# Low parts of weights on GpSimd, and gates, scan and query rows moved ahead, in the first block's input runs

## The reference, cut to what matters

```python
hn = rms_norm(h, norm_mix_g[l])
q, k, v, xr, gate = jnp.split(hn @ w_in[l], splits, axis=-1)      # five parts of 512 columns
q = apply_partial_rope(rms_norm(q, q_norm_g[l]), cos, sin)        # per head of 64; k alike
o_attn = diff_attention(q, k, v, lam)
xc = conv(xr)                                                     # width 4, causal
r = sigmoid(xb @ w_rg + b_rg); i = sigmoid(xb @ w_ig + b_ig)      # the two gates, in blocks of 64
a = exp(8 * r * log_sigmoid(lru_L))
u = sqrt(max(-expm1(2 log a), 0)) * i * xc
y = scan(a, u)                                                    # y[t] = a[t] * y[t-1] + u[t]
o_rec = rms_norm(y * gelu(gate), rec_norm_g[l])
h = h + concat(o_attn, o_rec) @ w_out[l]
```

## Time and profile before

| | us |
|---|---|
| median of 3 runs | 1753.96 (1753.67 to 1758.41) |
| the profiled execution | 1755.41 |
| its span | 1752.6 |
| TensorE busy, matmuls | 1629.3 (93%) |
| VectorE busy | 1014.0 (58%) |
| ScalarE busy | 843.1 (48%) |
| GpSimd busy | 21.0 (1%) |
| mean granted TensorE clock | 0.961 |

### The profile page before, as it was taken

One profiled execution on the slowest core, in us unless ns is written; L12 is line 12 of the kernel. 1 busy time (PEld: TensorE's weight loads), 2 busy tenths in 40 slices (PEclk: granted clock), 3 DMA queues, 4 the chain that ended last, 5 costly groups with the idle time before them and its releaser, 6 DMA issues.

```text
span 1752.6 us, 27456 instructions
## 1 busy us (share of the span) xinstructions
PE 1629.3 (93%) x11494; PEld 1421.4 (81%) x11494; DVE 1014.0 (58%) x1621; ACT 843.1 (48%) x1410; POOL 21.0 (1%) x38
## 2 busy tenths in 40 slices
PE   6978999989898999999989899999999798989997
PEld 6947999989578999887657778888887674779997
DVE  7675645465856555724453665325554666577575
ACT  6744434448445444534563454224432446556563
POOL 0000000000000000310000000000000000000000
PEclk9989999999898999999999899999999898989998
DMA  7445545353455463771102451232223520244632
GB/s 286 145 182 191 197 147 210 131 196 144 169 205 205 142 219 146 214 228 73 72 1 73 169 198 68 92 135 96 74 83 121 216 97 1 72 181 153 228 144 91
DMA packets 60522, 253.84 MB, mean 145 GB/s; under 512 B 4976, under 2 KB 8304, under 8 KB 42480
## 3 DMA queue, kind: packets, MB, share of 16 engines
q1 hardware_dynamic: 59088, 248.95, 38.6%
q0 software_dynamic: 1312, 3.15, 0.9%
HBM read 251.03 MB, written 1.05 MB: 144 GB/s over the span
## 4 chain that ended last, share of the span: by engine, by line
PE 63%; DVE 3%; ACT 2%; issue 1%; DVEq 0%; ACTq 0%
PE PA L849 49%; PE PA L910 2%; PE PA L911 2%; PE PB L1206 2%; PE PA L920 1%; PE PB L1193 1%; PE PB L790 1%; DVE small L1913 1%; PE PA L1379 1%; PE PA L1278 1%; PE PA L883 1%; PE PA L884 1%; PE PA L889 1%; DVE tmp L1613 1%; PE PB L979 1%
## 5 line engine op out<-in xcount | busy, mean ns | idle before, releaser
L1423 DVE TENSOR_TENSOR WL_t<-raw,WH_t 128x1024 fp32r<-128x1024 f32 (+1 forms) x344 | 444.5, 1297 | 370.1 <-ACT WH_t L2044 369.8
L849 PE MATMUL PA<-XH_t,WH_t 128*128 128x256 f32 (+2 forms) x1984 | 632.6, 319 | 8.4 <-issue 4.4
L849 PE MATMUL PA<-XL_t,WH_t 128*128 128x256 f32 (+2 forms) x1984 | 626.5, 316 | 0.0
L849 PE MATMUL PA<-XH_t,WL_t 128*128 128x256 f32 (+2 forms) x1984 | 626.3, 316 | 0.0
L2044 ACT ACTIVATE WH_t<-raw 128x1024 fp32r<-128x1024 f32 (+1 forms) x344 | 381.3, 1113 | 206.9 <-PE PA L849 171.2
L849 PEld LDWEIGHTS PA<-XH_t,WH_t 128*128 128x128 f32 x1984 | 379.3, 191 | 40.5 <-issue 14.6
L849 PEld LDWEIGHTS PA<-XL_t,WH_t 128*128 128x128 f32 x1984 | 379.5, 191 | 21.5 <-issue 0.5
L849 PEld LDWEIGHTS PA<-XH_t,WL_t 128*128 128x128 f32 x1984 | 379.2, 191 | 21.8
L849 PE MATMUL PA<-AH_t,WH_t 128*128 128x256 f32 (+2 forms) x616 | 192.0, 312 | 0.3 <-DVE AL_t L1446 0.2
L849 PE MATMUL PA<-AH_t,WL_t 128*128 128x256 f32 (+2 forms) x616 | 190.9, 310 | 0.0
L849 PE MATMUL PA<-AL_t,WH_t 128*128 128x256 f32 (+2 forms) x616 | 190.2, 309 | 0.0
(11 more groups left out here) (262 smaller groups left out, 1651.7 us busy)
## 6 DMA issues: line engine op xcount, KB each, us to landing
raw<-in_w_ada SPq DMA_DIRECT2D x48, 1024.0 KB, 5.0
raw<-in_w_gu SPq DMA_DIRECT2D x44, 1024.0 KB, 4.8
raw<-in_w_dn SPq DMA_DIRECT2D x64, 704.0 KB, 4.0
raw<-in_w_up SPq DMA_DIRECT2D x44, 1024.0 KB, 4.8
raw<-in_w_in SPq DMA_DIRECT2D x30, 1024.0 KB, 5.2
raw<-in_w_out SPq DMA_DIRECT2D x12, 1024.0 KB, 4.8
raw<-in_w_qkv SPq DMA_DIRECT2D x6, 1024.0 KB, 6.2
raw<-in_w_outc SPq DMA_DIRECT2D x4, 1024.0 KB, 6.0
```

Source lines behind the costliest of these rows:

```text
L849: mm = pe.matmul(PA[:, (L.b0 + o) % 4, 0:T], W[:, c:c + P], X[:, k, L.x0:L.x0 + T], start=(n == 0 and m == 0 and not L.early), stop=(n == ...
L1423: dve.tensor_tensor(WL_t[:, w:w + L.cols], RAWV[:, r % RAW, part * UNIT:part * UNIT + L.cols], WHf[:, w:w + L.cols], ALU.subtract).then_in ...
```

## The change

Five things change, all in the two layers of the first block, and the results are the same.

1. GpSimd makes the low parts of weights that are due during the second and the third input run (`a.pool`): tiles 8 to 19 and the first four tiles of the output projection, 16 a layer. VectorE's `splits` leaves them out. GpSimd's list of them comes ahead of its DMA issues.
2. The gates' second half goes behind tile 9 instead of 10. ScalarE's sigmoids, decay and the square of the decay follow there at once (stage 4), and VectorE makes the multiplier in stage 4 instead of behind tile 12.
3. The scan and the gated output move from stage 7 to stage 6, ScalarE's squares of it from 8 to 7, the sum over features a tile ahead on VectorE (17) and TensorE (18), its root from the end of the run to behind tile 18.
4. Behind tile 16 VectorE scales the keys ahead of the queries' reciprocal; the keys' reciprocal moves from tile 19 to 18.
5. The spread of the query roots moves from `mix1_pe` to behind tile 19, into `PB` instead of `PA`, and its product into `first_dve`. TensorE waits for that product at the start of attention, ahead of the first transposes of values.

```diff
+                a.pool = tile0 > 0
...
-                    if L.lru and L.lru[1] + s == 3:
-                        lru_gates(L.lru[0], 0)
+                    if L.lru and L.lru[1] + s in (3, 4):
+                        lru_gates(L.lru[0], L.lru[1] + s - 3)
...
-                if o == 10:
-                    lru_gates(l, 1)
-                elif o == 12:
+                if o == 12:
...
+
                     pe.wait_ge(S("lr_acc"), 3 * l + 3)
                     pe.matmul(PB[:, 1, 0:T1], ones, RG[:, 0, :], start=True, stop=True).then_inc(S("lr_sum"), 1)
+                elif o == 19:
+
+                    pe.wait_ge(S("qk_row"), 2 * l + 1)
+                    pe.wait_ge(S("qk_rt"), 2 * l + 2)
+                    pe.wait_ge(S("lr_rt"), l + 1)
+                    for i in range(4):
+                        mm = spread_rows(PB[:, i, :], 0, i)
+                    mm.then_inc(S("qk_bc"), 1)
...
-                pe.wait_ge(S("qk_row"), 2 * l + 1)
-                for i in range(4):
-                    mm = spread_rows(PA[:, i, :], 0, i)
-                mm.then_inc(S("qk_bc"), 1)
+                pe.wait_ge(S("qk_ready"), 2 * l + 1)
                 turn_values(0)
                 ada_sums(A.first, A.raw0)
...
-                        if L.outs * s + q >= L.ahead:
+                        if L.outs * s + q >= L.ahead and not L.pool:
                             for x in todo[q]:
                                 split_lo(*x)
...
                     last.then_inc(S("rotg"), 1)
+
+                    dve.wait_ge(S("lr_at"), l + 1)
+                    link(dve.scalar_tensor_tensor(TT, RG, 1.0, TT, ALU.add, ALU.mult))
+                    dve.tensor_scalar(TT, TT, 0.0, None, ALU.max).then_inc(S("lr_m2"), 1)
...
-                elif stage == 7:
                     for i in range(4):
                         last = dve.tensor_tensor_scan(XC[:, i, :], AA[:, i, :], IG[:, i, :], 0.0, ALU.mult, ALU.add)
...
                 elif o == 16:
+                    scaled(1)
                     inverse(0)
-                    scaled(1)
                 elif o == 17:
                     rotated(1)
+                    lru_dve(l, 10)
                 elif o == 18:
                     dve.wait_ge(S("qk_rh"), 2 * l + 1)
                     dve.tensor_tensor(RL[0], m1_row[0], RHf[0], ALU.subtract).then_inc(S("qk_row"), 1)
-                    lru_dve(l, 10)
+                    inverse(1)
                 elif o == 19:
-                    inverse(1)
+                    spread_product(l, 0)
...
+            def spread_product(l, g):
+
+
+                dve.wait_ge(S("qk_bc"), 2 * l + g + 1)
+                dve.tensor_tensor((QQ, KK)[g], TA[g], (PB, PA)[g][:, :, 0:T1], ALU.mult).then_inc(S("qk_ready"), 1)
...
-                elif stage == 5:
+                elif stage == 4:
+                    lru_gates(l, 1)
+                    lru_decay(l)
                     act.activation(RG, AA, ACT.Square).then_inc(S("lr_at"), 1)
...
+            for L in lins:
+                for s in range(L.n if L.pool else 0):
+                    for row in L.freed(0, s):
+                        for M, i, s1, q in row:
+                            r, part = M.chunk(s1, q)
+                            w = M.place(s1, q)
+
+                            pool.wait_ge(S("w_hi"), M.tile(i, s1, q))
+                            pool.tensor_tensor(WL_t[:, w:w + M.cols], RAWV[:, r % RAW, part * UNIT:part * UNIT + M.cols],
+                                               WHf[:, w:w + M.cols], ALU.subtract).then_inc(raw_done[r % RAW], M.units)
```

More of the change, by code:

```diff
@@ L240, in __init__ @@
                 self.ahead = 2 if inner and len(parts) == 1 else 0
+                self.pool = False
                 if inner:
@@ L1043, in first_pe @@
                     row_sums(PB[:, 0, :], bones[:, 48:80], SQ1[1], "qk_sum")
-                elif o == 19:
                     pe.wait_ge(S("lr_acc"), 3 * l + 3)
                     pe.matmul(PB[:, 1, 0:T1], ones, RG[:, 0, :], start=True, stop=True).then_inc(S("lr_sum"), 1)
+                elif o == 19:
[5 more added lines that the diff above has]
+                    mm.then_inc(S("qk_bc"), 1)
             def mix1_pe(l):
@@ L1074, in mix1_pe @@
                 pe.wait_ge(S("qk_row"), 2 * l + 2)
-                pe.wait_ge(S("qk_ready"), 2 * l + 1)
                 for i in range(4):
@@ L1761, in first_dve @@
                 if o == 12:
-                    dve.wait_ge(S("lr_at"), l + 1)
-                    link(dve.scalar_tensor_tensor(TT, RG, 1.0, TT, ALU.add, ALU.mult))
-                    dve.tensor_scalar(TT, TT, 0.0, None, ALU.max).then_inc(S("lr_m2"), 1)
                     dve.wait_ge(S("lr_g"), 2 * l + 2)
@@ L1778, in first_dve @@
                     dve.tensor_tensor(RL[0], m1_row[0], RHf[0], ALU.subtract).then_inc(S("qk_row"), 1)
-                    lru_dve(l, 10)
+                    inverse(1)
                 elif o == 19:
-                    inverse(1)
+                    spread_product(l, 0)
+            def spread_product(l, g):
+                dve.wait_ge(S("qk_bc"), 2 * l + g + 1)
+                dve.tensor_tensor((QQ, KK)[g], TA[g], (PB, PA)[g][:, :, 0:T1], ALU.mult).then_inc(S("qk_ready"), 1)
             def mix1_dve(l):
-                GG = [QQ, KK]
                 dve.wait_ge(S("qk_rh"), 2 * l + 2)
                 dve.tensor_tensor(RL[1], m1_row[1], RHf[1], ALU.subtract).then_inc(S("qk_row"), 1)
-                for g in range(2):
-                    dve.wait_ge(S("qk_bc"), 2 * l + g + 1)
-                    dve.tensor_tensor(GG[g], TA[g], PA[:, :, 0:T1], ALU.mult).then_inc(S("qk_ready"), 1)
+                spread_product(l, 1)
                 lru_dve(l, 11)
@@ L2302, in lru_act @@
                     act.activation(TT, TT, ACT.Sqrt).then_inc(S("lr_m"), 1)
-                elif stage == 8:
+                elif stage == 7:
                     act.wait_ge(S("lr_y"), l + 1)
                     act.activation(RG, GA, ACT.Square).then_inc(S("lr_sq"), 1)
-                elif stage == 9:
+                elif stage == 11:
                     act.wait_ge(S("lr_sum"), l + 1)
@@ L2334, in rooted @@
                     act.activation(m1_row[g], PB[:, 0, 0:T1], ACT.Sqrt, bias=eps, scale=1.0 / 64).then_inc(S("qk_rt"), 1)
-                if o == 10:
-                    lru_gates(l, 1)
-                    lru_decay(l)
-                elif o == 12:
+                if o == 12:
                     act.wait_ge(S("of_act"), L.a0 + 4)
@@ L2351, in first_act @@
                     rooted(1)
+                    lru_act(l, 11, None)
             def mix1_act(l):
```

## The result

The changed kernel takes 1772.47 us (median of 4 runs, 1771.05 to 1772.97) against 1754.11 for the kernel before beside it (4 runs, 1753.67 to 1758.41): 1.0098 times the time before, interval 1.008 to 1.0115. It is slower, by 18 us. The prediction was 1738.2 us with a range of 1729 to 1770: the time lies above the range and on the other side. It is near the time that rival C gave, 1769.3, and 3.2 us above it. The profiled execution took 1771.05 us, its span is 1769.3 (1752.6 before), the mean granted clock 0.963.

A forecast was written before the change was run, and what follows sets the result against it. TensorE was taken to bound the kernel, losing time only where it waits for VectorE or runs slowly. Savings of 20.8 us less 5.0 of hindrance gave 15.8, so 1753.96 became 1738.2 us; range 1729 to 1770.

The forecast's parts named there:

- rival C: Input runs: each waiting GpSimd subtraction goes ahead of VectorE for its whole 2.4 us; 15.3 us slower, 1769.3; chance 0.24.
- the sum: Both layers, no hindrance between engines: 8.7 us saved in layer 0, 8.0 in layer 1, 4.1 by the clock: 20.8.
- The waits that stay: TensorE: 0.9 us at the gates, 1.5 at the spread product, 0.3 at the scores in layer 0; 1.8 in layer 1.
- the low clock: Tile 19, behind the key row sums' wait: slow matmuls cost 1.9 us in layer 0 and 2.2 in layer 1.
- The subtraction's price: One GpSimd low part: taken as 2.4 us, between 1.2 and 6.9, and hidden at that length.
- Does GpSimd hinder VectorE? I take half for the forecast.: Shared SBUF, mainly at the convolution: half of each subtraction's 2.4 us added to VectorE's chain, 5.0 us in all.
- case A: Input runs: GpSimd doesn't hinder VectorE at all; the whole 20.8 us saved, 1733.2; chance 0.20.
- VectorE's row operations of 0.4 us can slip between: Convolution: short VectorE operations fit between GpSimd's subtractions, a reason given for counting only half the hindrance.
- The row-sum chain absorbs the rest in its 3 us: VectorE ahead of the key row sums: ends about 3 us before tile 18 does, which covers the remaining hindrance.
- the 0.5 us a layer for the low part of the key roots: End of the run: the key roots' low part meets the last GpSimd subtractions, costing 0.5 us a layer.
- B: Input runs: exclusion with VectorE first, GpSimd falls behind and tile 17 waits; 6.8 us saved, 1747.2; chance 0.18.
- Case D: GpSimd paces the tiles if a subtraction exceeds 3.9 us; at 5 us about 5 us lost a layer, 1764; chance 0.06.

The follow-up runs named there:

- the 8-element kernel: The changed kernel with each GpSimd subtraction cut from 1024 elements to 8, most of those low parts left unmade; 1733.6 us, ratio 0.9888.

## Why the prediction was wrong, point by point

**What bounds the kernel.** Right. TensorE waits for VectorE in these places, and with that taken away and nothing put in its place (the 8-element kernel) 19.7 to 20.8 us are to be had; the sum said 20.8. That it agrees so well is luck, for two terms in it were off in opposite directions. The waits that stay are 3.5 us in layer 0 and 2.5 in layer 1, not 2.7 and 1.8, since the scores wait 0.83 rather than 0.3, the query rotation 0.2 rather than nothing, and layer 0's gates 1.02 rather than 0.9 (the spread product's 1.50 was foreseen). And the low clock was sized too small: TensorE is busy for 53.0 and 51.8 us in the windows before and for 48.5 and 48.4 with short instructions, 8.0 us in all where 4.1 was reckoned. The 4.1 came from the tile behind the 4.1 us wait alone. The granted clock was 0.56 in the first tile behind layer 0's gates too (46.7 to 49.7 us) and 0.50 from the key spread to the scores of either layer (105.14 to 107.4 and 466.5 to 468.8). These terms make 23 us; the two profiled spans differ by 22.5, the medians by less.

**The subtraction's price.** Right: 2.39 us alone, 2.4 taken.

**"Does GpSimd hinder VectorE? I take half for the forecast."** This is the step that failed: the hindrance was put at 5.0 us, and it is 39 us from the 8-element kernel to the changed one. The ends were nothing and the whole 2.4 us on VectorE's chain, and the middle was taken for want of a row near either. The convolution shows which end it was: 9.42 us with two subtractions, where case C had 10, the forecast 8 and case A 5.3. Half had no mechanism behind it: that "VectorE's row operations of 0.4 us can slip between" is true (each gets its turn) and doesn't help, since GpSimd then takes a turn of 2.4 us as long as a subtraction is ready. "The row-sum chain absorbs the rest in its 3 us" failed with it: with 8-element instructions VectorE is done 2.7 us ahead of the end of tile 18 (82.5 and 85.2 us), so the cover was there, and with whole subtractions it comes 3.8 us too late. Only the 0.5 us a layer for the low part of the key roots came about as priced (0.57 us ahead of the key spread). Here the Trainium skill (SBUF — State Buffer, Who interferes with whom) states what the runs show: a two-input operation of VectorE and a reading one of GpSimd exclude each other for the whole instruction, and one that only writes doesn't count (the convolution takes 9.42 us beside two subtractions and 5.27 beside two fills). The prediction had it at hand, gave it 0.42 in B and C, and let a mean of the bounds stand as the likeliest case.

**Rival C, place by place.** Waits of 5.8, 5.3, 4.9 and 2.1 us were laid out; 4.76, 3.84, 6.48 and 2.90 came, with 0.17: 18.2 us against 18.1. The mechanism is right; that the sums agree to 0.1 us is partly luck, since single places are off by 0.8 to 1.6 us. The convolution loses 2.1 us for each subtraction, not 2.4 (two of its operations take 2.5 and 2.6 us, the other ten 0.49); why not the whole, no run tested. The loss moved from the row sums to the recurrent sum, where three short additions of 1.39 us together take 5.43 with two subtractions between them. Its 1.9 us for the clock came as 1.7. C, as its citation, spoke of operations with two inputs; the one with one input and a constant (line 1724, 0.73 to 2.91 us) is held up as well.

**The moves.** By themselves they save nothing (1756.2): the prediction's order of work holds only once VectorE is freed. With GpSimd in the way, the recurrent sum, now due a tile sooner, is the longest wait of all, 6.48 us. The prediction's forecast has no term for it; with the splits back on VectorE and no GpSimd it is 1.62 us already.

**Case D** played no part. No tile waits for GpSimd in the changed kernel; two a layer do once its subtractions are made in quarters. Its own sum doesn't follow from its terms: 80 us against 61, less a saving of 8 to 9, is some 10 us lost a layer and not 5.

**The chances.** B, VectorE first, did not occur with whole subtractions, but the quarters come near it: VectorE keeps most of the time and tiles wait for GpSimd.

## What to carry to other kernels

Before work goes from VectorE to an idle GpSimd, ask which operations of VectorE run in the same stretch. With two inputs in SBUF each of them can wait for one whole GpSimd instruction, so price the move as that wait times the number of turns on the chain that is due, and not as a fraction. That is what these runs show for the sizes of this kernel. If the move is wanted, cut GpSimd's instructions to a length that the chain can bear, keep them away from series of short VectorE operations, and try first whether postponing the same work in VectorE's own list gives as much: here both gave 0.6%, each with steps moved ahead.

## What the runs showed of the hardware that was not expected

- Busy time contains waiting for the other engine. VectorE's busy total rose by 10.7 us with 39 us of work taken off it; a held operation shows as a long one, with no idle time and no releaser in the trace. The sign to look for is one form with two durations (line 1728: 1.29 and 3.23 us).
- The two engines take turns, even where one has a series ready back to back: six subtractions of 2.39 us took 18.82 us, and the convolution's twelve operations took 9.42 us in place of 5.27 beside two subtractions, with one operation slipped in between.
- Cutting 2.39 us into four costs 0.44 us alone (2.83), and made the kernel 20 us faster.
- A fill by GpSimd, which reads nothing, leaves VectorE's two-input operations alone but lengthens its operation with one input and a constant (0.73 to 1.46 us). Why this one is held up by writing, no run tested. The operations of 1088 elements with an input in PSUM stayed at 1.23 to 1.29 us in every kernel.
